# Rows of experts moved from the top-k lanes to places in the mixer

## Time and profile before

| what | us |
|---|---|
| median of 3 runs (4250.11 to 4257.94) | 4251.03 |
| profiled execution | 4220.8 |
| its span, first to last instruction | 4219.0 |
| DVE busy | 3237.9 |
| POOL busy | 2447.4 |
| PE busy | 1839.2 |
| ACT busy | 431.3 |
| mean DMA rate | 307 GB/s |

### The profile page before, as it was taken

How to read it: one execution, slowest core, us unless ns; L and a number is a source line. 1 busy time by engine, 2 the same in 40 slices (tenths; PEclk the granted TensorE clock), 3 DMA queues, 4 the chain that set the end, 5 groups by cost and what they waited for, 6 DMA issues and landing times. The chain is left out here.

```text
span 4219.0 us, 26743 instructions
## 1 busy us (share of the span) xinstructions
PE 1839.2 (44%) x7808; PEld 1445.5 (34%) x7808; DVE 3237.9 (77%) x5899; ACT 431.3 (10%) x954; POOL 2447.4 (58%) x2052
## 2 busy tenths in 40 slices
PE   8799410085788311037579511009669811100000
PEld 6576300064576211025367411006458511000000
DVE  2211799966666989977777789987576699998999
ACT  2210000022110000002210000002221000000000
POOL 0000577856455487765557467766455557778776
PEclk9889755598899655568789755559879955555555
DMA  4233799978789799889789879888778989989998
GB/s 176 75 110 122 256 363 344 342 279 327 249 318 394 270 347 345 329 305 365 277 314 409 333 280 354 330 335 317 281 279 337 356 307 346 325 318 321 385 408 357
DMA packets 359890, 1295.61 MB, mean 307 GB/s; under 512 B 40512, under 2 KB 40768, under 8 KB 359744
## 3 DMA queue, kind: packets, MB, share of 16 engines
q0 software_dynamic: 294912, 1073.87, 68.1%
q1 hardware_dynamic: 64256, 217.94, 14.1%
q10 hardware_dynamic: 576, 2.10, 0.1%
HBM read 1291.65 MB, written 2.10 MB: 307 GB/s over the span
## 5 line engine op out<-in xcount | busy, mean ns | idle before, releaser
L977 POOL DMA_INDIRECT ring<-in_peer_u,eidx x1024 | 1315.9, 1285 | 1066.4 <-DVE eidx L1087 521.0
L977 POOL DMA_INDIRECT ring<-in_peer_v,eidx x1024 | 1131.3, 1105 | 686.0 <-DVE acc L1017 310.9
L1017 DVE SCALAR_TENSOR_TENSOR acc<-ring,wgt,acc 128x1024 f32<-128x1024 f32 x1024 | 1269.6, 1289 | 42.2 <-DMA ring<-in_peer_v,eidx 38.4
L1012 DVE CUSTOM_DVE_ANT_0 ring<-ring,hp 128x1024 f32<-128x1024 f32 x1024 | 1209.2, 1221 | 101.4 <-DMA ring<-in_peer_u,eidx 95.8
L485 PE MATMUL bank<-xt,panel 128*128 128x256 f32 x4096 | 959.0, 394 | 54.5 <-ACT work L783 30.2
L485 PEld LDWEIGHTS bank<-xt,panel 128*128 128x128 f32 x4096 | 809.0, 199 | 180.5 <-ACT work L783 31.8
L717 PE MATMUL bank<-panel,yt 128*128 128x128 f32 x256 | 47.0, 312 | 784.6 <-ACT yt L921 384.3
L717 PEld LDWEIGHTS bank<-panel,yt 128*128 128x128 f32 x256 | 40.9, 213 | 793.7 <-issue 788.4
L497 PE MATMUL bank<-cst,work 128*128 128x128 f32 x64 | 12.8, 368 | 644.3 <-ACT xt L765 637.0
L1233 DVE TENSOR_REDUCE nmax<-bank 128x1 f32<-128x128 f32 (+3 forms) x128 | 62.4, 487 | 233.7 <-PE bank L539 233.7
L497 PEld LDWEIGHTS bank<-cst,work 128*128 128x128 f32 x64 | 10.6, 193 | 645.3 <-issue 638.0
(11 more groups left out here) (160 smaller groups left out, 1832.9 us busy)
## 6 DMA issues: line engine op xcount, KB each, us to landing
panel<-in_panels SPq DMA_DIRECT2D x368, 512.0 KB, 6.7
ring<-in_peer_u,eidx POOLq DMA_INDIRECT x1024, 6.5
ring<-in_peer_v,eidx POOLq DMA_INDIRECT x1024, 6.5
work<-in_rel_bias SPq DMA_DIRECT2D x16, 512.0 KB, 7.8
gb<-in_ln_g SPq DMA_DIRECT2D x8, 512.0 KB, 6.9
gb<-in_ln_b SPq DMA_DIRECT2D x8, 512.0 KB, 8.5
panel<-in_keys SPq DMA_DIRECT2D x16, 256.0 KB, 6.1
work<-in_x SPq DMA_DIRECT2D x4, 512.0 KB, 5.5
```

Of the source, the lines that this page charges most:

```text
L977: pool.indirect_dma_start(ring[:, n % RING, :], None, t_in["peer_u" if kind == "U" else "peer_v"], bass.IndirectOffsetOnAxis(ap=eidx[:, t, ...
L1012: v.tensor_tensor_reduce(row, row, hp[:, t, :], 1.0, 0.0, ALU.mult, ALU.add, hid[:, t, c:c + 1]).then_inc(used, 1)
L1017: stt(out=acc[:, t, :], in0=row, scalar=wgt[:, t, c:c + 1], in1=acc[:, t, :], op0=ALU.mult, op1=ALU.add).then_inc(used, 1)
```

## The change

A lane gets 56 rows instead of 80. The numbers of the mixer's rows are now written out: `MIXER_ROWS` gives for A and C a block ahead of the first unit and the rows of the units (16 and 60; 16 and 56), for B what the first slot has on top and the rest (8 and 40), 8 under a new key R, 64 in G, and 12 added to the 16 of the old key L, which is now called O. The blocks of A and C stand on DVE before the wait for the first scores and before the first rotary product, R before the reciprocal of `rms`. ACT's `gelus` calls stand at the matching points. Lane 0 keeps its 48 rows; the tail has what is left of the last phase, 512 - 3 x 56 = 344 rows. `finish` waits on the count of the last V row.

```diff
-LANE_ROWS = 80
+LANE_ROWS = 56
+MIXER_ROWS = {"A": (16, 60), "B": (8, 40), "C": (16, 56), "R": 8, "G": 64, "O": 12}
@@ row_plan, for each phase s > 0
-            left = ROWS - LAST - 3 * LANE_ROWS
-            share = {"A": left * 10 // 40, "B": left * 7 // 40, "C": left * 10 // 40}
-            share["G"] = left - sum(share.values())
-            for u, n in enumerate(spread(share["A"], UNITS)):
-                plan += [((s, "A", u, i), k) for i, k in enumerate(spread(n, 5))]
-            for j, n in enumerate(spread(share["B"], 2)):
-                plan += [((s, "B", j, i), k) for i, k in enumerate(spread(n, 4))]
-            for u, n in enumerate(spread(share["C"], UNITS)):
-                plan += [((s, "C", u, i), k) for i, k in enumerate(spread(n, 5))]
-            plan += [((s, "G", x, 0), k) for x, k in enumerate(spread(share["G"], 12))]
-            plan.append(((s, "L", 0, 0), LAST // 4))
+            for stage in "AC":
+                before, total = MIXER_ROWS[stage]
+                if stage == "C":
+                    early, later = MIXER_ROWS["B"]
+                    for j, n in enumerate(spread(later, 2)):
+                        plan += [((s, "B", j, i), k + (early if i + j == 0 else 0)) for i, k in enumerate(spread(n, 4))]
+                plan.append(((s, stage, -1, 0), before))
+                for u, n in enumerate(spread(total, UNITS)):
+                    plan += [((s, stage, u, i), k) for i, k in enumerate(spread(n, 5))]
+            plan.append(((s, "R", 0, 0), MIXER_ROWS["R"]))
+            plan += [((s, "G", x, 0), k) for x, k in enumerate(spread(MIXER_ROWS["G"], 12))]
+            plan.append(((s, "O", 0, 0), MIXER_ROWS["O"] + LAST // 4))
@@ ACT
             def stage_a(s):
+                gelus((s, "A", -1, 0))
                 take_qk("A", s, 0)
@@
                 act.wait_ge(b_done, (s + 1) * 2)
+                gelus((s, "C", -1, 0))
                 take_qk("C", s, 0)
@@
+                gelus((s, "R", 0, 0))
                 act.wait_ge(o_ev["C"], (s + 1) * UNITS)
@@
-                gelus((s, "L", 0, 0))
+                gelus((s, "O", 0, 0))
@@ DVE, rope
                 if u == 0:
                     dve.wait_ge(tables, 1)
+                if u == 0:
+                    rows((s, "C", -1, 0))
                 dve.wait_ge(qk_ev["C"], n + 1)
@@ DVE, attention_stage
                 if kind == "C":
                     rope(s, 0)
+                else:
+                    rows((s, "A", -1, 0))
@@ DVE, rms
+                rows((s, "R", 0, 0))
                 dve.wait_ge(rms_root, s + 1)
@@ DVE, mixer_norm and finish
-                rows((s, "L", 0, 0))
+                rows((s, "O", 0, 0))
...
-                dve.wait_ge(used, (p + 1) * ROWS)
+                dve.wait_ge(used, max(last_sum.values()) + 1)
```

## The result

| | us |
|---|---|
| after, median of 4 runs (4059.35 to 4065.75) | 4061.22 |
| before beside it, median of 4 runs (4250.11 to 4258.27) | 4254.48 |
| ratio, 95% interval | 0.9554 (0.9532 to 0.9577) |
| profiled execution after (span 4059.8) | 4061.6 |

The kernel is 4.5% faster; the forecast was 4084 us. The two profiled executions differ by 159 us, the medians by 193, because the profiled one of before was some 34 us under its median and that of after is at it.

The account below looks back on a forecast made before the run. DVE was taken to bound the top-k lanes, the PE-ACT-DVE chain the mixers, row supply second. Lanes -378, mixers +115 and tail +96 made -167 us: 4054 profiled, 4084 us with the 30 us median difference, range 4030 to 4150.

Parts of the forecast that it names:

- The sum: Whole kernel: lanes -378, mixers +115, tail +96, together -167 us, giving 4084 us.
- Lanes: 24 rows fewer in each of twelve lanes: -338 us of rows, -40 of waits, -378 us in all (-338 to -405).
- Blocks: 16 U rows ahead of stages A and C, 20.9 us each, would fit into DVE's waits for PE.
- My margin of 0.9 us in C: Stage C: block and rotation end at 1071.0, PE's value projection at 1071.85, so the block is covered.
- the even mixer's A and C: Phase 2's mixer: unit rows cost 7.2 us in A, 4.8 in C; supply adds 4 plus 2 in A, 2 in C.
- B: Stage B: first slot's added rows fill DVE's 14.09 us wait down to some 4; other slots +3.6 us, supply +3.
- R, G, O: Mixer's last stages: R +1.3 us (odd phases) or +4.8 (even), plus 1 for supply; G and O together +10.3.
- Tail: the mis-sized term: 72 more rows in the tail at 1.33 us each: +96 us (83 to 111), start-up taken as already paid.
- The 30 us between profiled execution and median: Before's median of 4251.03 us lay 30 us above its profiled execution; carried over, 4054 became 4084 us.
- The supply did not bound the mixers: Rival, mixers: supply bounds them, 216 moved rows at 1.90 us cost 410 us; 4379 us, chance 0.04.
- The rows were hidden: Against the rival that mixer rows are not hidden and cost 257 us; 4226 us, chance 0.10.
- The V-row rival: O and tail: V rows in long runs hold POOL up, +14 us a mixer, +21 in the tail; 4147 us, chance 0.03.

## Why the prediction was right, point by point

- **The sum.** -159 us in the profiled executions for a forecast of -167 looks closer than its terms are. The lanes came out 27 us better than forecast, the tail 33 us worse, the mixers 6 us worse, and 5 us came from the mixer of phase 0. That the first two cancel is luck.
- **Lanes.** Row by row as forecast: 94.8 us in lane 1 for 95, and no lane waited for its scores. The term came out at its far end, -405 for -378. The waits for U rows fell by 49 us (67.1 to 17.7; I took 40), and the removed rows cost more than I priced: -405 less 338 and 49 leaves 18 us. Single rows between top-k steps don't overlap their neighbours as rows back to back do; at the instruction's own mean of 1.22 and 1.29 us, 160 U and 128 V rows make 360 us and not 338. That last step is worked out, not tested.
- **Blocks.** Both cover themselves, shown by taking each away: 52 us for A's three, 67 us for C's, though some 3 us of waiting remain at the first maximum. My margin of 0.9 us in C held: PE's value projection ended 3.5, 3.0 and 0.5 us after DVE's rotation in the three phases. What I got wrong is the even mixer's A and C (+18.6 and +13.7 us; I had 13.2 and 6.8) and A of phase 3 (+16.0; I had 10.2). No experiment separates that.
- **B.** The wait went from 14.09 to 8.23 us and not to 4 (5.81 and 9.23 in the others), yet the stage grew by 4 to 6 us, as forecast (6.6).
- **R, G, O.** Together +13.3 us in phase 1; I had 2.3 + 0 + 10.3. O's 12 rows cost 12.1 us, 1.0 us each, as rows that nothing hides; O ran at 409 GB/s and took 46.9 us for 45.
- **Tail: the mis-sized term.** I priced a row at 1.33 us; between the two profiled executions it was 129.4/72 = 1.80. Part of the cause is in my own rows: POOL's 1.73 us beside U rows. I treated the tail's 1.54 us as a start-up that is paid once, but slow stretches come back later in the tail. 9.6 us are the one wait that is not for a row. The rest hangs on which executions are compared: 272 rows took 375.6, 396.0 and 370.4 us in three executions, 344 rows without the gap 466 to 511. On one chip the tail went from 396.0 us (80 rows a lane) to 502.3 (mean of the three kernels with 56), +106 us or 1.48 a row; on another from 370.4 to 466.2, +96 us or 1.33, which is my price. So how wrong the price was beyond this pair stays open.
- **The 30 us between profiled execution and median.** I carried them over; after has no such difference. Without them the forecast would have read 4054, and 4061 was measured. Where the profiled execution of before was quick its one trace can't tell; only the tail was seen to vary by that much.
- **The rivals.** The supply did not bound the mixers (a moved row cost 121/216 = 0.56 us). The rows were hidden, if not wholly. The V-row rival came true in neither place: O's 12 V rows cost 12.1 us and not 24. But V rows do hold POOL up by some (1.30 us an issue, 0.94 beside one input), which I took as absent from 17 issues beside V rows that were not back to back.

## What to carry to other kernels

Filler work goes where its engine waits for others, in blocks that end before the waited-for result, and each block needs its supply there already. Check what hangs on the block's last item in other engines' programs: one row made the difference between 0.993 and 0.986 here. When a consumer's instructions hold its producer up, a consumer slowed a little can lose nothing and wait no more (tails of 457 us for 466 to 477 on the same chips); and the time of a stage that varies from execution to execution is read from several traces, on the same chip, before anything is credited to an edit.

## What the runs showed of the hardware

- POOL's indirect issue beside DVE's rows under 1.22 us apart: 1.73 us with the two-input dot product, 1.30 with the two-input accumulation, 0.94 with a one-input sum. A gap of 0.23 us between dot products brings it to 1.07.
- With that gap V rows were used at 1.25 us each, faster than 0.524 MB can come at 409 GB/s (1.28 us). The DMA itself did not go faster: it moved 409 GB/s in the middle of such a stretch. The rows came from what the ring had gained beside the slower U rows.

```profile
3960.00:3990.00 30.00, 0.00 (x0) 0.00 (x0) 30.00 (x26) 0.00 (x0) 21.63 (x23) 0.50 1.03 409
```

- The tail, whose 344 rows and their order are the same in seven of the kernels, took from 466 to 511 us in their profiled executions (one of them with the ring of 12: 469). The long ones spent more of it at 1.4 us a row, the short ones at 1.28; chance and chip are not separated.
